# A four-layer fp32 network on one core: layer borders worked in halves of 256 tokens, with the norms as tasks of the next layer's plan

## The reference: what is computed

```
x = even_layer(x)    # rms norm, 8 sliding-window + 8 relative-bias heads, x + y @ w_out
x = odd_layer(x)     # rms norm, differential attention, x + y @ w_out
for i in (0, 1):     # ALPHA = 4 ** 0.25
    mix = ssd_mixer(h) if i == 0 else mla_attention(h)    # neither norms its input first
    h = layer_norm(ALPHA * h + mix, ln_mix_g[i], ln_mix_b[i])
    ff = conv_ffn(h)                                      # 1024 -> 2 x 2816 -> 1024, conv of 3 taps, silu gate
    h = layer_norm(ALPHA * h + ff, ln_ffn_g[i], ln_ffn_b[i])
```

## Time and profile before

| | us |
|---|---|
| runs (3) | 2171.59, 2172.98, 2173.01 |
| median | 2172.98 |
| profiled execution, its own time | 2174.18 |
| its span on the core | 2172.4 |
| PE busy in the span | 2044.9 |
| mean granted TensorE clock | 0.974 of full speed |

### The profile page before, as it was taken

The page is one execution under the profiler, slowest core; times in us unless marked ns, Lnnn a source line. Parts: engine busy times, 40 slices in busy tenths (PEclk is TensorE's granted clock), DMA queues, the critical chain, the costliest instruction groups (busy, mean ns, idle before and its releaser), DMA issues.

```text
span 2172.4 us, 24614 instructions
## 1 busy us (share of the span) xinstructions
PE 2044.9 (94%) x9666; PEld 1653.1 (76%) x9666; DVE 1045.0 (48%) x1765; ACT 949.2 (44%) x1597; POOL 784.8 (36%) x365
## 2 busy tenths in 40 slices
PE   6999989999999999999896999999799969999996
PEld 4878867877778888888685878888568857888885
DVE  3374552376655555565535464412436564444205
ACT  4355534366634444555324444422445444444223
POOL 2422234333243333332343444444432334444443
PEclk9999999999999999999997999999899979999998
DMA  4211122211122222212221323333111212333331
GB/s 173 87 40 49 41 86 78 78 49 49 49 80 76 68 65 72 69 59 69 68 78 49 102 88 97 95 97 90 58 46 39 78 49 88 97 97 97 97 90 56
DMA packets 47491, 162.49 MB, mean 75 GB/s; under 512 B 5392, under 2 KB 8080, under 8 KB 47248
## 3 DMA queue, kind: packets, MB, share of 16 engines
q1 hardware_dynamic: 46944, 159.54, 22.9%
q10 hardware_dynamic: 432, 1.39, 0.2%
HBM read 158.80 MB, written 2.10 MB: 74 GB/s over the span
## 4 chain that ended last, share of the span: by engine, by line
PE 88%; DVE 7%; ACT 3%; issue 1%; DMA 0%; POOL 0%; ACTq 0%; DVEq 0%
PE ps L1671 23%; PE ps L1674 23%; PE ps L1672 23%; PE ps L1708 3%; PE ps L1723 3%; PE ps L1692 2%; PE ps L1716 1%; PE ps L1800 1%; PE ps L1790 1%; PE ps L1686 1%; PE ps L1685 1%; PE ps L1683 1%; PE ps L1697 1%; PE ps L1702 1%; DVE res L2320 1%
## 5 line engine op out<-in xcount | busy, mean ns | idle before, releaser
L2387 POOL TENSOR_TENSOR wl<-st,wh 128x1024 fp32r<-128x1024 f32 (+2 forms) x311 | 714.0, 2298 | 1295.1 <-ACT wh L1822 1295.1
L1671 PE MATMUL ps<-xh,wh 128*128 128x512 f32 x1512 | 624.5, 413 | 48.2 <-DVE xl L2324 28.2
L1674 PE MATMUL ps<-xh,wl 128*128 128x512 f32 x1512 | 596.1, 394 | 0.0
L1672 PE MATMUL ps<-xl,wh 128*128 128x512 f32 x1512 | 595.2, 394 | 0.0
L1822 ACT ACTIVATE wh<-st 128x1024 fp32r<-128x1024 f32 (+2 forms) x311 | 313.6, 1010 | 596.6 <-PE ps L1674 554.5
L1671 PEld LDWEIGHTS ps<-xh,wh 128*128 128x128 f32 x1512 | 288.4, 191 | 120.5 <-DVE xl L2324 32.9
L1674 PEld LDWEIGHTS ps<-xh,wl 128*128 128x128 f32 x1512 | 287.6, 190 | 62.8
L1672 PEld LDWEIGHTS ps<-xl,wh 128*128 128x128 f32 x1512 | 288.7, 191 | 58.6 <-issue 5.3
L2346 DVE SCALAR_TENSOR_TENSOR tmp<-ps,vec,tmp 128x510 f32<-128x510 f32 (+1 forms) x176 | 131.4, 749 | 253.7 <-ACT tmp L2002 250.7
L2304 DVE SCALAR_TENSOR_TENSOR res<-res,ps 128x512 f32<-128x512 f32 x32 | 21.8, 685 | 248.7 <-PE ps L1674 248.7
L1671 PE MATMUL ps<-fa_h,wh 128*128 128x512 f32 x352 | 139.8, 397 | 0.0
(11 more groups left out here) (255 smaller groups left out, 3048.2 us busy)
## 6 DMA issues: line engine op xcount, KB each, us to landing
st<-in_f_up SPq DMA_DIRECT2D x88, 512.0 KB, 3.4
st<-in_s_xbc SPq DMA_DIRECT2D x32, 512.0 KB, 3.4
st<-in_f_dn SPq DMA_DIRECT2D x32, 512.0 KB, 3.5
st<-in_o_fm SPq DMA_DIRECT2D x24, 512.0 KB, 3.5
st<-in_e_fm SPq DMA_DIRECT2D x21, 512.0 KB, 3.4
st<-in_s_z SPq DMA_DIRECT2D x16, 512.0 KB, 3.4
st<-in_s_out SPq DMA_DIRECT2D x16, 512.0 KB, 3.3
st<-in_f_dn SPq DMA_DIRECT2D x16, 384.0 KB, 3.1
```

The costliest lines, as they stand in the source:

```text
L1671: e.matmul(u.bank.ap, hi, x.h[:, kk, :], start=first, stop=False)
L1672: e.matmul(u.bank.ap, hi, x.l[:, kk, :], start=False, stop=False)
L1674: e.matmul(u.bank.ap, lo, x.h[:, kk, :], start=False, stop=last).then_inc(S["mm"], 1)
L2387: e.tensor_tensor(P.mem["wl"][w.m % NWR][:, 0:w.n], P.mem["stage"][w.m % NSTAGE][:, 0:w.n], P.mem["wh"][w.m % NWR][:, 0:w.n].bitcast(F32), ...
```

## The change

1. **Last units in halves.** `outputs` works its last unit (the last two in the even layer and mla) as tokens 0 to 255 over all k, then tokens 256 to 511 (`proj_halves_g`, kind `mm_half`, L1805, L1806, L1808).
2. **Norms in halves, as tasks.** `LayerNorm` and `SquareNorm` replace `LayerStats`, `layer_norm`, `SquareStats` and `rms`. `half(i)` runs the statistics, the root and the eight output tiles of one half. These tasks are marked `last`: `run` returns while they are still open, and the next layer's `run` goes on with them. The pivot is taken after 4 tiles, not 5.
3. **First units in halves.** `proj_border_g` works the next layer's first three units, whichever half of whichever tile is there (instead of a pair).
4. **Other places for operands.** Centring by the mean moves from DVE and POOL to DVE alone and reads mean and pivot from PSUM; the root is written to PSUM.
5. **Side changes.** The feed-forward has 4 unit banks instead of 2; mla's latents, its values and the ssd's `dt` steps become tasks; `x` arrives in halves, the first weights between them; each output DMA takes 2 tiles x 256 tokens.

```diff
-    def rms(self, srcs, toks, gcol, n, eps, H, L, freed, bank=None):
-    def layer_norm(self, st, gcol, bcol, H, L, freed):
-class LayerStats:
-class SquareStats:
+    def proj_border_g(self, x, srcs, done):
+        banks = Ring(self.pj.slots + ([] if len(self.pj.slots) > 2 else [self.slots[7]]))
+        ns, us, at, total = [self.ask(s) for s in srcs], [], [], srcs[0].shape[1]
...
+        def due():
+            return next(((i, j) for i in range(2) for j, a in enumerate(at)
+                         if a[i] < total and x.half[i][a[i]] is not None), None)
...
+            us[j].done = w.used = yield ("mm_half", us[j], w, k, x, k, i, k == 0, k == total - 1)
+    def proj_halves_g(self, x, srcs, done):
+        for i in range(2):
+            for j, parts in enumerate(srcs):
...
+                        u.done = w.used = yield ("mm_half", u, w, k, x, kk, i, kk == 0, kk == total - 1)
+                    w.over = i == 1
+class LayerNorm:
+    def half(self, i, toks):
+        for k in range(self.k0, 8):
+            c[k] = yield ("cen", x, pivot, self.pivot_t, toks[k], [], 256)
+            q = yield ("csq", part(s), s.use.freed, x, c[k], 256)
+            t = yield ("shift", shift, [], shift, x, c[k], shift_t, 256)
+            a = yield ("acc", acc, part(s), acc_t, [q], 256)
...
+        tm = yield ("ones", part(mean), mean.freed, shift, shift_t, True, True, 256)
+        ts = yield ("ones", part(sq), sq.freed, acc, acc_t, True, True, 256)
+        t = yield ("msq", d, self.d.use.freed, part(mean), tm, 256)
+        v = yield ("var", d, part(sq), t, ts, 256)
+        a = yield ("ln", d, d, 1.0, P.c(C_E5, 1), [v], [], 256)
+        r = yield ("rs", part(sq), d, a, 256)
+        for k in range(11):
+            if k < 8:
+                cen[k] = yield ("ln_cen", x, part(mean), [t, tm], c[k], after.get(k) or self.after[k], 256)
+            if 0 < k < 9:
+                scaled[j] = yield ("ln_mul", x, part(sq), r, cen[j], 256)
+                kept[j] = yield ("ln_out", x, self.gain(j), self.bias(j), scaled[j], 256)
+                    hi[j] = yield ("ln_hi", x, self.x.h[:, j, cs], kept[j], self.freed, 256)
+            if k > 2 and self.x is not None:
+                lo = yield ("ln_lo", res[:, j, cs], self.x.h[:, j, cs], self.x.l[:, j, cs], hi[j], 256)
-def outputs(P, y, srcs, evac, stats, third=lambda: [], wide=3, begin=None):
+def outputs(P, y, srcs, evac, norm, third=lambda: [], wide=3, halves=1, begin=None):
+        yield from norm.whole(k0)
+        for i in range(2):
+            P.start(3, norm.half(i, parts[i]), True)
-    for j in range(wide, 8):
+    for j in range(wide, k0):
         u = yield from P.proj_g(y, srcs(j))
         P.start(2, post(j, u))
+    yield from P.proj_halves_g(y, [srcs(j) for j in range(k0, 8)], lambda i, j, u: P.start(2, post_half(i, j, u)))
 def run(self, *gens):
-        while self.tasks:
+        while any(not (t.last and gens) for t in self.tasks):
 def ffn(P, layer, x, kept, norm, over):
+    pj2, P.pj = P.pj, Ring([P.slots[i] for i in (0, 1, 7, 3)])
-                for c, u in zip((0, 22), (yield from P.proj_pair_g(x, [T["f_up"][layer, c] for c in (0, 22)]))):
-                    P.start(2, post(c, u))
+        first = (0, 22, 1)
+        yield from P.proj_border_g(x, [T["f_up"][layer, c] for c in first], lambda j, u: P.start(2, post(first[j], u)))
```

More of the change, by code:

```diff
@@ L149, with __init__, over @@
     done: tuple = None
-@dataclass
 class Acts:
-    h: object
-    l: object
-    t: list
+    def __init__(self, h, l, n):
+        self.h, self.l, self.t, self.half = h, l, [None] * n, ([None] * n, [None] * n)
+    def over(self, k, step, i=None):
+        for j in (0, 1) if i is None else (i,):
+            self.half[j][k] = step
+        if self.half[0][k] is not None and self.half[1][k] is not None:
+            self.t[k] = [self.half[0][k], self.half[1][k]]
 @dataclass
 class Task:
-    rank: int
+    rank: float
     gen: object
+    last: bool = False
     step: object = None
     ready: float = 0.0
-def now(*steps):
-    for s in steps:
-        yield s
 class Plan:
@@ L642, in add @@
         self.tok[k] = tok
-        if k == 0:
-            while not P.at.free(3):
-                yield lambda: P.at.free(3)
-            self.pivot, self.mean, self.sq = (Use(s) for s in P.at.slots)
-            self.acc, self.squares = None, []
         if k == 1:
@@ L717, in follow, with half @@
+    def half(self, i, toks):
+        P, cs = self.P, HALF[i]
+        part = lambda b: b.ap[:, cs]
+        acc, acc_t, done = part(self.acc), self.acc_t, list(self.toks)
+        for k in range(self.k0, 8):
             while toks[k] is None:
                 yield lambda: toks[k] is not None
-            yield from stats.add(k, toks[k])
+            s, done[k] = self.s[k - self.k0], toks[k]
+            q = yield ("sq", part(s), s.use.freed, self.res[:, k, cs], toks[k], 256)
+            a = yield ("acc", acc, part(s), acc_t, [q], 256)
+            acc_t = [a]
+            s.release(a)
+        bank = yield from P.taken(Ring([P.slots[3 + i]]))
+        t = yield ("ones", part(bank), bank.freed, acc, acc_t, True, True, 256)
+        self.acc.release(t)
+        yield from P.rms_g(bank, t, [self.res[:, k, cs] for k in range(8)], done, self.gain, self.x, self.freed, i)
@@ new lines, in outputs, with follow @@
+def outputs(P, y, srcs, evac, norm, third=lambda: [], wide=3, halves=1, begin=None):
+    k0 = 8 - halves
+    toks, parts = [None] * k0, ([None] * 8, [None] * 8)
+    both = [[] for _ in range(halves)]
+    def follow():
+        for k in range(k0):
+            while toks[k] is None:
+                yield lambda: toks[k] is not None
+            yield from norm.add(k, toks[k])
+        yield from norm.whole(k0)
+        for i in range(2):
+            P.start(3, norm.half(i, parts[i]), True)
@@ L726, in outputs @@
         begin()
+    if norm.freed is None:
+        norm.freed = P.fence()
     P.start(3, follow())
@@ L854, in stream @@
     def stream():
+        yield from P.proj_border_g(x, [w[j] for j in range(3)], lambda j, u: P.start(4, gates.first(j, u)))
+        P.start(4, gates.first(3, (yield from P.proj_g(x, [w[3]]))))
         yield from prep(0, 12, "a_kn", True, "k", ks)
@@ L873, in stream @@
                 P.start(5, gates.bring(j, u))
-        rt.append((yield from outputs(P, y, lambda j: [T["e_out"][j]], evac, sums, third)))
+        rt.extend((yield from outputs(P, y, lambda j: [T["e_out"][j]], evac, norm, third, halves=2)))
     def finish(fb, ob, mn, sm, ends):
@@ L1132, with ssd @@
     gate_t: list
-def ssd(P, xt, over):
+def ssd(P, x, norm, over):
     mem, T = P.mem, P.T
@@ L1352, in stream, with first @@
                     P.start(5, z_in(got[g - 1], j, u))
-        yield from outputs(P, y, lambda j: [T["s_out"][j][:, 0:8], T["s_out"][j][:, 8:16]], evac, stats, begin=begin)
+        yield from outputs(P, y, lambda j: [T["s_out"][j][:, 0:8], T["s_out"][j][:, 8:16]], evac, norm, begin=begin)
+    def first(j, u):
+        P.start(4, conv(got[0], 1 + j, 8 + 8 * j, u) if j else steps(u))
     def begin():
@@ L1444, in rotation, with mla @@
     P.rope_ready = [t1, t2]
-def mla(P, x, kept, over):
+def mla(P, x, kept, norm, over):
     mem, T = P.mem, P.T
@@ L1506, in q_post @@
     def q_post(h, u):
-        q = yield from P.taken(qn)
+        q = yield from P.taken(rings["m_qn"])
         hi, lo = q.ap
@@ L1538, in stream @@
                     P.start(4, v_post(b, 1, us[b]))
-        yield from outputs(P, y, lambda j: [T["m_out"][j]], evac, stats, third)
+        yield from outputs(P, y, lambda j: [T["m_out"][j]], evac, norm, third, halves=2)
     caus = P.c(C_CAUS)
@@ L1687, in pe_program @@
         elif kind == "ones":
-            bank, x, ready, first, last = o
+            out, freed, x, ready, first, last, n = o
             if first:
-                pe.freed(bank)
+                pe.wait_ge(freed)
             pe.wait_ge(ready)
-            e.matmul(bank.ap, ones, x.ap, start=first, stop=last).then_inc(S["ones"], 1)
+            e.matmul(out, ones, x, start=first, stop=last, skip_group_check=True).then_inc(S["ones"], 1)
         elif kind == "blk":
```

717 lines of the change are left out of this document (378 added, 339 removed).

## The result

The median of 4 runs is 2102.47 us (2100.85 to 2102.87), beside 2172.99 (2171.59 to 2174.46) of the kernel before: ratio 0.9674, 95% interval 0.9657 to 0.9691. The forecast was 2114 (2094 to 2142).

The account below looks back on a forecast made before the run. PE bounds the layers and loses time at their borders: 115.7 us of losses before, 56.4 after, 59.3 saved. 2174.2 - 59.3 - 1.2 = 2113.7, so 2114 us (2094 to 2142).

Parts of the forecast that it names:

- The after side: Losses at layer borders, start and tail left after the change: 56.4 us in sum.
- in-order waits that a list by hand does not show: At four borders, an allowance of 1 us each that no row prices: 4 us.
- The gaps of a border: PE's idle at ssd to feed-forward 0: 1.6 + 2.9 + 0.9 + 0.3 = 5.7 us.
- The clock: Clock loss at borders after the change: 1.5 us at ssd to feed-forward 0, 0.5 at even to odd.
- The splitting: Matmuls of 512 columns run as two halves: 11 ns more a pair, 8 us for the 732 pairs.
- The taps: PE's waits in the feed-forward for conv taps to free a bank: 10.5 us, with 4.8 of clock, would go.
- then the latents' norms: 16 us with 12.59 busy (3.4): Feed-forward 0 to mla, before the change: 3.4 us lost at the latents' norms, part of that border's 22.8.
- the before side: Losses of the kernel before at layer borders, taps and tail, against PE at full speed: 115.7 us.
- all hidden: Rival, chance 0.12: the gaps at the borders close and the clock stays up, 2084 us.
- The ports: Rival, chance 0.20: POOL's weight steps hold DVE's two-SBUF-source steps, 7 us more at each of four borders, 2142.
- The rival on the load: Rival, chance 0.04: the 191 ns weight load sets each half matmul's pace, 105 us more, 2219.
- the rival in which the halves don't part: Rival, chance 0.04: a weight slot or bank keeps first units back until the second half is there, 2166.

Follow-up runs that it names:

- four other kernels with the same gaps: The changed kernel with one edit each: two banks (2107.8 us), odd border whole (2100.5), latents' norms in series (2111.5), feed-forward bodies in halves (2131.0).
- The series run: The changed kernel with the two norms of mla's latents again as steps of the unit stream, as before the change: 2111.5 us.

## Why the prediction was right, and what it mis-sized

The sign and, in the main, the mechanism were right. Point by point:

- **The after side** was forecast as 56.4 us of losses. The same count from the trace (from the last unit's first half matmul to the first units' last, each half at 0.2273 / 2 us) gives even to odd 36.54 - 240 x 0.1137 = 9.3 (forecast 7.5), odd to ssd 1.7 (1.5), ssd 8.6 (10.3), feed-forward 0 to mla 7.0 (10.0), mla to feed-forward 1 11.1 (10.5), tail 12.8 and 1.6 of splitting and first half's ones (13.6 in all): 52.1, less 0.3 at the start: 51.8. So 4.6 too much, and that is about the 4 for in-order waits that a list by hand does not show: no such waits were seen.
- **The gaps of a border.** Forecast for the ssd border: idle 1.6, then 2.9 before the second half's ones, then 0.9 for a weight. Measured 1.31, 1.79 and none, and the 1.79 is behind a step that POOL held, as forecast (an `acc`, not a `shift`). Elsewhere the list fits less well: at feed-forward 0 to mla the first gap is 1.39 for a low weight, then 1.53 for a held `shift`; at mla to feed-forward 1 there is none before the first tile, but 3.92 before the ones; at even to odd both gaps, 1.11 and 2.19, are behind `xl` steps that POOL held, and not behind the lambda steps.
- **The clock** was taken as 1.5 a border. It was 0.91 of full speed for 18 us at the ssd border and 0.90 for 16.5 at mla's, about 1.6 each; nothing at feed-forward 0 to mla, where four other kernels with the same gaps have 1.6 or more; 0.76 for 12.9 us at even, 3.1 where I had 0.5.
- **The tail**: 12.8 from the last matmul against 12.9 forecast.
- **The splitting**: 13.3 to 14.5 ns a pair against 11, so 10 us for 732 pairs, not 8.
- **The taps** were counted as 10.5 of waits and 4.8 of clock. In the kernel before, four banks give 17.7, so 2.4 more; in the changed kernel, either edit does most of it.
- **The step that was most off in size** is "then the latents' norms: 16 us with 12.59 busy (3.4)" in the before side. Those 16 us hold the wait of 0.5 and 2.9 of the 3.3 before `m_cql`. Left out were a wait of 1.2 before ones at 1575, the last 0.4, and the low clock behind the long wait, 1.7 in these 4.6 us:

```profile
1606.38:1611.00 4.62, 4.62 (x13) 3.67 (x14) 2.44 (x4) 0.94 (x3) 1.35 (x1) 0.63 0.11 28
```

That makes 6.7, 3.3 more than counted, and 1.0 of short waits for `m_pt` went with it. The series run, with 7 to 8 us that are the latents', agrees with the two together. So of the 8.3 us of surplus in this stretch some 4.3 are the before side and 3.0 the after side (7.0 for 10.0).

Taken together, the before side comes to 115.7 + 2.4 + 4.3 = 122.4, and 122.4 - 51.8 = 70.6 of the 71.8 between the spans; 1.2 stays open. Both sides erred the same way, so nothing cancelled; the result is inside the range because that reached 20 us below the forecast.

Of the rivals, all hidden (2084) would have needed no gap, and 7.9 + 1.8 + 1.7 + 1.4 + 3.3 less the tail's 1.6 = 14.5 us of waits were left. The ports are real: POOL held two steps at even to odd, one at ssd, three at feed-forward 0 to mla, two at mla to feed-forward 1, where I had counted two a border and the rival three. Their price of 7 us a border did not come: PE's gaps stayed at 3 to 5 us a border, and the clock cost 3.1 at even, 1.6 or nothing elsewhere. The rival on the load needed 0.16 us a half matmul, and it is 0.12. And PE does start on the first half while the second is under way, so the rival in which the halves don't part falls.
